# A transformer pair on one core: mixer stages merged into one program, seams and a row fetch moved

## The reference

```python
gate = one_hot(group) * within          # two of 16 experts per row
for e in range(16):
    hid = silu(t @ w1[e]) * (t @ w3[e])
    out = out + gate[:, e:e + 1] * (hid @ w2[e])
x = x + g_f * out
```

```python
x = layernorm(ALPHA * x + 0.5 * swiglu(x, w_gate, w_up, w_down))   # D_FF 2816
x = layernorm(ALPHA * x + mixer(x))
x = layernorm(ALPHA * x + 0.5 * swiglu(x, ...))
```

## Time and profile before

| | us |
|---|---|
| median of 3 runs | 2616.94 (2616.81 to 2618.58) |
| the profiled execution | 2617.32 |
| its span, first to last instruction | 2615.5 |
| PE busy in the span | 2465.8 (94%) |
| DVE, ACT, POOL busy | 1412.0, 1013.5, 54.3 |
| granted TensorE clock, mean | 0.976 of full |

### The profile page before, as it was taken

How to read it: one execution, slowest core, us unless ns; L and a number is a source line. 1 busy time by engine, 2 the same in 40 slices (tenths; PEclk the granted TensorE clock), 3 DMA queues, 4 the chain that set the end, 5 groups by cost and what they waited for, 6 DMA issues and landing times. The chain is left out here.

```text
span 2615.5 us, 33377 instructions
## 1 busy us (share of the span) xinstructions
PE 2465.8 (94%) x12238; PEld 2051.4 (78%) x12238; DVE 1412.0 (54%) x2055; ACT 1013.5 (39%) x1448; POOL 54.3 (2%) x84
## 2 busy tenths in 40 slices
PE   7998959999699999998999999999999988999998
PEld 4877837888588888786798888888888867988886
DVE  5887578999643332588733323533323786533324
ACT  6345347777422221246332222222222454322211
POOL 0011010000100000000000000000000000000000
PEclk9999979999899999999999999999999999999999
DMA  6764659999643332330333334323323312333332
GB/s 241 284 214 141 258 222 370 402 407 403 255 120 96 96 96 91 99 88 33 97 97 96 96 97 119 91 78 97 97 90 105 92 57 65 97 90 96 97 95 73
DMA packets 310486, 381.62 MB, mean 146 GB/s; under 512 B 14540, under 2 KB 227180, under 8 KB 310262
## 3 DMA queue, kind: packets, MB, share of 16 engines
q1 hardware_dynamic: 300744, 345.10, 39.7%
q0 software_dynamic: 6896, 26.22, 2.6%
q10 hardware_dynamic: 2750, 8.99, 0.8%
HBM read 346.17 MB, written 34.10 MB: 145 GB/s over the span
## 5 line engine op out<-in xcount | busy, mean ns | idle before, releaser
L1656 DVE TENSOR_TENSOR w_part_lo<-w_raw,w_part_hi 128x1024 fp32r<-128x1024 f32 x252 | 308.3, 1225 | 734.3 <-ACT w_part_hi L1652 733.5
L1652 ACT ACTIVATE w_part_hi<-w_raw 128x1024 fp32r<-128x1024 f32 x252 | 266.9, 1062 | 794.5 <-PE PS L1662 760.2
L1660 PE MATMUL PS<-xT_hi,w_part_hi 128*128 128x512 f32 (+1 forms) x1472 | 556.7, 378 | 14.2 <-PEq L1928 8.3
L1661 PE MATMUL PS<-xT_lo,w_part_hi 128*128 128x512 f32 (+1 forms) x1472 | 555.0, 377 | 0.0
L1662 PE MATMUL PS<-xT_hi,w_part_lo 128*128 128x512 f32 (+1 forms) x1472 | 555.0, 377 | 0.0
L1660 PEld LDWEIGHTS PS<-xT_hi,w_part_hi 128*128 128x128 f32 x1472 | 279.8, 190 | 67.8 <-DVE w_part_lo L1656 15.7
L1661 PEld LDWEIGHTS PS<-xT_lo,w_part_hi 128*128 128x128 f32 x1472 | 279.5, 190 | 50.1 <-issue 0.2
L1662 PEld LDWEIGHTS PS<-xT_hi,w_part_lo 128*128 128x128 f32 x1472 | 279.6, 190 | 49.9
L1660 PE MATMUL PS<-w_part_hi,h_hi 128*128 128x512 f32 x576 | 228.1, 396 | 0.0
L1661 PE MATMUL PS<-w_part_lo,h_hi 128*128 128x512 f32 x576 | 227.8, 395 | 0.0
L1662 PE MATMUL PS<-w_part_hi,h_lo 128*128 128x512 f32 x576 | 227.8, 395 | 0.0
(11 more groups left out here) (470 smaller groups left out, 4052.4 us busy)
## 6 DMA issues: line engine op xcount, KB each, us to landing
expert_w_raw<-in_w SPq DMA_DIRECT2D x136, 512.0 KB, 7.3
w_raw<-in_ffn_w_gate SPq DMA_DIRECT2D x88, 512.0 KB, 3.8
w_raw<-in_ffn_w_up SPq DMA_DIRECT2D x88, 512.0 KB, 3.8
w_raw<-in_ffn_w_down SPq DMA_DIRECT2D x88, 512.0 KB, 3.8
w_raw<-in_w SPq DMA_DIRECT2D x68, 512.0 KB, 6.3
w_raw<-in_w_in SPq DMA_DIRECT2D x56, 512.0 KB, 4.8
late_raw<-in_w_ada SPq DMA_DIRECT2D x32, 512.0 KB, 5.7
w_raw<-in_w_out SPq DMA_DIRECT2D x24, 512.0 KB, 4.8
```

Of the source, the lines that this page charges most:

```text
L1652: nc.scalar.activation(t.hi, raw[t.n % 4], ACT.Copy).then_inc(w_hi, 1)
L1656: nc.vector.tensor_tensor(t.lo, raw[t.n % 4], t.hi.bitcast(f32), ALU.subtract).then_inc(w_lo, 1)
L1660: nc.tensor.matmul(out, a[0][a_at], b[0][b_at], start=first, stop=False, skip_group_check=True)
L1661: nc.tensor.matmul(out, a[0][a_at], b[1][b_at], start=False, stop=False, skip_group_check=True)
```

## The change

- **Router**: for each block of 128 rows, the rows (`hfT`) are the weights and the 20 router columns move; the logits come out with rows on partitions, so the bias is added by DVE in the copy that it made anyway; ACT's step and the four small transposes go. The bias is loaded to all 128 partitions.
- **Row fetch**: the eight gathers are issued at the end of the expert section, behind POOL's wait for `e_all`, not in the section after it. One of the two additions for row block 2 is done before the turned rows are copied out.
- **Seams after a feed-forward**: `ahead.tiles[1]` is split at the start of the next section, ahead of the norm of blocks 2 and 3, not at the end of the old one.
- **Mixer**: the three sections are one. The heads are done in an order (`OF`) after which the 128-column chunks of `o_tok` are complete in pairs of heads; three of four are turned (`o_turn`) and two are copied out inside the head loop. Tile 0 of `w_out` is split in the loop too. POOL's product is behind a wait for the gates.
- **Last feed-forward**: the last six down tiles are used three times, for blocks 0 and 1, for 2, for 3, and the norms of blocks 2 and 3 are done singly.

```diff
-            for kc in range(KC):
-                pe.wait_ge(q_ev_v if kc % 2 else q_ev, kc // 2 + 1)
-                last = nc.tensor.matmul(PS[0:20, 0, :], rw[:, kc, :], hfT[:, kc, :], start=kc == 0, stop=kc == KC - 1)
-            last.then_inc(q_lgT, 1)
-            pe.wait_ge(q_lgT_out, 1)
             for b in range(TB):
-                last = nc.tensor.transpose(PS[:, 1, b * 20:(b + 1) * 20], lgT[:, b * P:(b + 1) * P], ident[0:20, 0:20])
+                for kc in range(KC):
+                    if b == 0:
+                        pe.wait_ge(q_ev_v if kc % 2 else q_ev, kc // 2 + 1)
+                    last = nc.tensor.matmul(PS[:, 0, b * 20:(b + 1) * 20], hfT[:, kc, b * P:(b + 1) * P], rw[:, kc, :], start=kc == 0, stop=kc == KC - 1)
             last.then_inc(q_lg, 1)
...
             dve.wait_ge(q_lg, 1)
-            V.tensor_copy(lg.rearrange("p s e -> p (s e)"), PS[:, 1, 0:SETS * 4])
+            TT(..., PS[:, 0, 0:SETS * 4]..., rb_row[:, :].unsqueeze(1).to_broadcast([P, TB, 20]), ALU.add)
...
             pool.wait_ge(e_all, 1)
+            for b in range(TB):
+                for k in range(2):
+                    nc.gpsimd.indirect_dma_start(out=raw_more[:, 2 * b + k, :], ..., in_=ys[:, :], ...).then_inc(S.y_in[b], 16)
...
             added(0)
             added(1)
+            added(2, (0,))
             for kc in range(KC):
                 turn_dve(dve, 0, 0, kc)
-            added(2)
+            added(2, (1,))
             added(3)
...
# ffn: ACT and DVE, end of a section; and start of the next
                         for kc in range(KC):
                             turn_dve(dve, s + 1, 0, kc)
                             if kc == 3:
                                 split_lo(ahead.tiles[0])
-                        split_lo(ahead.tiles[1])
...
+                        if s - 1 not in MIXERS:
+                            split_lo(T(1))
                         ln_sums_dve(dve, 1)
...
# ffn, the last one
-                        dve.wait_ge(w_used, T(N_FFN - 1).used)
-                        ln_sums_dve(dve, 1)
-                        ln_finish_dve(dve, s, 1, rows_final)
+                        for i in range(2):
+                            dve.wait_ge(*((w_used, T(N_FFN - 1).used) if i else (third_done, 1)))
+                            ln_sums_dve(dve, 1, (2 + i,))
+                            ln_finish_dve(dve, s, 1, rows_final, (2 + i,), i)
...
+                    if final:
+                        for n in range(N_DOWN - 6, N_DOWN):
+                            last = down(n, (2,))
+                        last.then_inc(third_done, 1)
...
# mixer, PE
+                    def o_turn(k):
+                        kc = O_ORDER[k]
+                        for b in range(TB):
+                            last = nc.tensor.transpose(PS[:, k, b * P:(b + 1) * P], o_tok[:, b, kc * P:(kc + 1) * P], ident[:, :])
+                        last.then_inc(m["otr_done"], 1)
...
+                    for u in range(QH + 1):
+                        if u + 1 < QH:
+                            scores(u + 1)
+                        if u == QH - 1:
+                            pe.wait_ge(m["scores_read"], U + QH - 1)
+                            pe.wait_ge(m["o_out"], U + 4)
+                            o_turn(0)
+                            o_turn(1)
+                        if u == QH:
+                            pe.wait_ge(m["scores_read"], U + QH)
+                            pe.wait_ge(m["o_out"], U + 6)
+                            o_turn(2)
+                        if u < QH:
+                            prob_transposes(u)
...
+                    pe.wait_ge(m["o_out"], U + QH)
+                    o_turn(3)
...
# mixer, ACT and DVE in the head loop
+                        if u == 6:
+                            split_hi(TO(0))
+                        if u == 7:
+                            y_hi(0)
+                            y_hi(1)
...
+                        if u == 7:
+                            split_lo(TO(0))
+                        if u == 8:
+                            y_lo(0)
+                            y_lo(1)
```

More of the change, by code:

```diff
@@ L135, in shared @@
     S.w_hi, S.w_lo, S.w_used = sem("w_hi_ready"), sem("w_lo_ready"), sem("w_used")
+    S.y_in = [sem(f"y_rows{b}") for b in range(TB)]
     return S
@@ L2204, in _ @@
                     norm_rows(sp, s)
+                    for n in range(4):
+                        load_tile(sp, Unplaced(TO(0).n + n), mout_src(l, n))
+                    for n in range(4, N_MOUT):
+                        load_tile(sp, TO(n), mout_src(l, n))
+                    ahead.load(sp)
                 @block.gpsimd
@@ new lines, in outputs @@
+                    def outputs(u):
+                        pe.wait_ge(m["pt_out0"], U + u + 1)
+                        pe.wait_ge(m["pt_out1"], U + u + 1)
+                        if u >= 2:
+                            pe.wait_ge(m["o_out"], U + u - 1)
+                        elif u == 1:
+                            pe.wait_ge(m["std_out"], l + 1)
+                        for b in range(TB):
+                            for j in range(1 if b == 0 else 0, 2):
+                                last = nc.tensor.matmul(PS[:, 6 + u % 2, b * P:(b + 1) * P], pT[:, u % 2, j, b, :], vt[:, b - 1 + j, :],
+                                                        start=j == 0 or b == 0, stop=j == 1, skip_group_check=True)
+                        last.then_inc(m["o_done"], 1)
@@ new lines, in _, with out_rows @@
+                    pe.wait_ge(m["o_out"], U + QH)
+                    o_turn(3)
+                    def out_rows(n, blocks, start, stop):
+                        half, kp = n // 4, MOUT_ORDER[n % 4]
+                        t = TO(n)
+                        pe.wait_ge(w_lo, t.made)
+                        if n < 2:
+                            pe.wait_ge(m["y_ready"], l * 4 + n + 3)
+                        if n == 2:
+                            pe.wait_ge(m["conv_ready"], l + 1)
+                        if n == 4:
+                            pe.wait_ge(m["y_ready"], l * 4 + 4)
+                        for b in blocks:
+                            for kk in range(2):
+                                last = product(PS[:, (0 if half else 4) + b, :], XT, (slice(None), 2 * kp + kk, slice(b * P, (b + 1) * P)), (t.hi, t.lo), (slice(None), slice(kk * HALF, (kk + 1) * HALF)),
+                                               n == start and kk == 0, n == stop and kk == 1)
+                        last.then_inc(w_used, 1)
@@ L2338, in _ @@
+                    act.wait_ge(m["o_done"], U + QH)
+                    for n in range(3, N_MOUT):
+                        split_hi(TO(n))
+                    ln_root_act(act, s, 0)
+                    split_hi(ahead.tiles[0])
+                    for kc in range(KC):
+                        turn_act(act, s + 1, 0, kc)
+                        if kc == 3:
+                            split_hi(ahead.tiles[1])
                 @block.vector
```

349 lines of the change are left out of this document (144 added, 205 removed).

## The result

The changed kernel takes 2625.88 us (median of 8 runs, 2623.31 to 2627.47) against 2618.15 before (8 runs): ratio 1.0027, 95% interval 1.0017 to 1.0038. It is 0.3% slower, and 5 us above the upper end of the predicted range. Its profiled execution has a span of 2622.7 us, 7.2 more than before.

What follows compares the result with a forecast made beforehand. PE is busy 94% of the span, so only its gaps can be won. Terms +9.5 - 0.7 - 9.9 + 4.4 - 1.5 - 3.8 = -2.0 us, from the median 2616.94 to 2615 us; range, 8 in 10, 2604 to 2621.

Steps and rivals of the forecast that it cites:

- One named a true part: Rival, chance 0.12: row fetch takes 18.4 us from the first gather, term +15.0; 2620.5 us alone.
- the scatters' tail: Row fetch: POOL's drain ends 2.9 us after the gathers, as it did behind five scatters.
- Step 1: Row fetch at the experts' closing barrier: POOL's drain holds the barrier and SP's loads; +9.5 us.
- Step 2: Router: 64 short matmul records at 0.11 us replace 16 long ones; -0.7 us.
- Step 3: Mixers, between projection and attention: without the barrier DVE's split and taps' sum follow each other; -0.65 us each, twice.
- Step 4: Mixers, head turns: most chunks turned early, so the first `w_out` product comes 4.8 us sooner; -4.3 us each, twice.
- Step 5: Two seams from a feed-forward to a mixer: norm 0.76 us later, turns at half clock 1.45 more; +4.4 us together.
- Step 6: Seam from feed-forward 2 to 3: PE starts 1.47 us sooner, the later norm comes just in time; -1.5 us.
- Step 7: End: after the last matmul DVE works on one block instead of two; -3.8 us.

Runs made afterwards that it cites:

- experiment 2: Kernel before with the row fetch moved and each gather fetching half-length rows; executed once for its trace: POOL's drain 13.2 us instead of 15.3 to 15.8.
- experiment 3: Changed kernel with POOL's multiplication waiting until DVE has read the taps' sum: 2619.2 us, ratio to before 1.0003.
- experiment 6: Changed kernel with fetch and router as before, POOL's multiplication held, norm's sums ahead of the second tile's split before mixers: 2599.8 us, 0.9935 of before.
- experiment 8: Experiment 6 plus 128-column router products, first feed-forward tiles loaded in the experts' section, norm first before feed-forward 3 too: 2596.9 us, 0.9920 of before.

## Why the prediction was wrong

**The result.** Faster, same and slower had 0.36, 0.55 and 0.09; it came slower by 0.27%, at 2625.9 where 2615 was forecast. No single rival gives it. One named a true part, that the fetch costs more than the scatters' tail says; but it took 18.4 us from the first gather where 15.6 came (706.20 to 721.80), and by itself it ended at 2620.5. The steps below show three that failed: the length of the drain, the clock under the router's products, and what the barrier in front of the scores had held back.

**Step 1, the fetch: right in mechanism, 2.4 short.** POOL's drain held the barrier and SP's loads queued behind it. The step that failed is "2.9 us of drain come after", taken from five scatters: behind the last gather's issue 5.8 came. The drain follows the data: eight gathers move 4.19 MB, and experiment 2 shows the length changing with the bytes. The Trainium skill, DMA: Bandwidth & Descriptors, section Anatomy of one DMA — SWDGE (gpsimd) path, says that of a DMA's fixed cost of about 2 us most is the receipt of its last byte; here about 1 us lies between the end of the traffic and the end of the drain, which fits in kind. From SP's load to the second turns it was 35.1 us where 38.5 had been before and 35.3 was forecast (13.44 and 23.20 less 1.3).

**Step 2, the router: wrong sign.** "48 at 0.11 end near 353.3" supposed one clock throughout. The pace was right for 20 records in 2 us and then the clock fell. The bound of 0.13 a record allowed for something slower, but the 0.149 over all lay outside. That the half clock was carried on into the experts' stretch I can't show: that stretch is 345.9 us on average in the three profiles with the changed router and 346.2 in the seven with the old.

**Step 3, projection to attention: the worst step, 4.1 off over both mixers.** It priced the barrier that goes (0.65 a mixer; with POOL held, experiment 3 measures 0.6 and 1.4) and not the instruction that the barrier had held: "Without the barrier they follow each other" looked at DVE's own list alone. The merging of the programs let POOL's multiplication run beside DVE's products. The Trainium skill, SBUF — State Buffer, section SBUF: two separate sides, says that GpSimd and VectorE share one pair of ports as an exclusive lock when VectorE has two operands in SBUF and GpSimd reads SBUF too; the numbers agree: the products, both of whose operands are in SBUF, lost 2.19 us to an instruction of 2.35, while the taps' sum, one of whose operands is in PSUM, took the same in both cases: 1.29 with POOL's instruction beside it before (1199.34 and 1199.42), 1.28 alone after. That POOL's instruction stretched the products is shown by experiment 3; that the ports are the reason is the Trainium skill's account, which no run here can separate from another.

**Step 4, head turns: right, -10.3 for -8.6.** The first `w_out` product follows the last heads as forecast. In mixer 1 it is -4.6 for the forecast -4.3. The surplus is -5.7 in mixer 4, which was not read for the forecast: in the kernel before half clock lasted there into the first `w_out` products,

```profile
2188.00:2190.00 2.00, 2.00 (x8) 0.50 0.78 302
2190.00:2192.00 2.00, 2.00 (x8) 0.73 0.00 0
```

(PE busy, clock, DMA share, GB/s), so that its stretch took 87.08 us against 85.67 in mixer 1, while the changed kernel's two are alike.

**Step 5, the seams: right, 4.6 for 4.4,** with both parts: turns 0.8 later (21.82 behind the last turns, 21.03 before) and half clock behind the wait. The wait was 3.62 us where 4.3 was forecast, and the 16 turns took 2.75 in mixer 1 (clock 0.69 over 1128 to 1131) and 3.36 in mixer 4. What I missed is that the two hang together (experiment 6).

**Step 6: -0.6 for -1.5.** The norm was not "just in time": PE waited 0.91 for it and 1.02 for the first hidden tile. With the norm first it is -2.0 (experiment 8).

**Step 7, the end: exact.**

**The 1.2 us left over** lie in the experts' stretch, which ranged from 343.7 to 349.7 in the twelve profiles (343.7 to 349.7 with the old router, 344.2 to 346.8 with the changed one). They can't be told from chance.

## What to carry to other kernels

Before merging two programs or taking a barrier away, list for each engine the first instruction that it had held, and look at what that instruction will now run beside; the engine off the critical path is the one to ask about. Don't put indirect gathers ahead of a barrier that others wait at: POOL's drain waits for their data, while SP's loads went ahead of it without holding it up. Where a long wait of PE was split into two short ones, the clock behind it stayed up; look for this before pricing a wait. A matmul with few moving columns can be cheaper with padding.

## What the runs showed of the hardware that was not expected

- PE's clock fell to 0.50 with no gap in PE's records, during matmuls of 128 weight columns and 20 moving ones; with 128 moving ones it stayed up, and the records took 0.115 and 0.121 instead of 0.149 us.
- A drain of POOL behind eight gathers took 13.2 us for 2.10 MB and 15.3 to 15.8 for 4.19 MB; a drain of SP 0.4 us behind its last load took 0.13, one of POOL with none in flight 0.30.
- Four products of DVE took 5.09 instead of 2.90 us beside one multiplication on POOL, all of it in one of them; held back, the same multiplication met a DVE instruction of 128 x 2 values, which took 1.90 instead of 0.23.
- PE's waits of 3.6 us in front of 16 turns left half clock in them (a window from 1128 on had 0.69), waits of 1.05 and 1.50 none; a wait of 3.05 was followed by half clock in one profile and by full clock in another.
- The experts' stretch varied by 6 us over the profiles of twelve kernels on the same data, ten of which differ in it by the router alone or not at all; what sets that is open.
